# The first token tile scaled by ScalarE, two Sin calls moved into the layer, and the last tile routed ahead of its low part, in a two-layer hybrid transformer kernel on Trainium2

## What is computed

```python
for l in range(2):
    h = rms_norm(x, norm_mix_g[l])
    q, k_c, v_c, k_s, v_s, k_w, v_w, nsa_g, sgu_in, s5_in, branch_g = split(h @ w_in[l])
    y_a = nsa_attention(q, k_c, ..., positions, ...) @ w_attn_o[l]   # partial_rope: cos/sin of positions
    y_b = spatial_gating(sgu_in, ...) @ w_sgu_o[l]
    y_c = s5_layer(s5_in, ...) @ w_s5_o[l]
    g_a, g_b, g_c = split(sigmoid(branch_g))
    x = x + (g_a * y_a + g_b * y_b + g_c * y_c) @ w_mix_o[l]
    h = rms_norm(x, norm_ffn_g[l])
    # 4 groups x 8 experts, the best group, its best 2 experts per token, silu(h Wg) * (h Wu) @ Wd
    x = x + hierarchical_moe(h, ...)
return rms_norm(x, norm_final_g)
```

## Time and profile before

| | us |
|---|---|
| median of 3 runs | 1911.43 (1910.63 to 1912.46) |
| the profiled execution, its device time | 1910.96 |
| its span in the trace | 1909.2 |
| PE busy | 1848.6 (97%), 10376 records |
| DVE busy | 990.3 (52%) |
| ACT busy | 483.7 (25%) |
| POOL busy | 151.2 (8%) |
| mean granted TensorE clock | 0.99 of full |
| read from HBM | 476.59 MB |

### The profile page before, as it was taken

The page is one execution under the profiler, slowest core; times in us unless marked ns, Lnnn a source line. Parts: engine busy times, 40 slices in busy tenths (PEclk is TensorE's granted clock), DMA queues, the critical chain, the costliest instruction groups (busy, mean ns, idle before and its releaser), DMA issues. The chain is left out here.

```text
span 1909.2 us, 26714 instructions
## 1 busy us (share of the span) xinstructions
PE 1848.6 (97%) x10376; PEld 1156.9 (61%) x10377; DVE 990.3 (52%) x1929; ACT 483.7 (25%) x858; POOL 151.2 (8%) x241
## 2 busy tenths in 40 slices
PE   6999999999999999999889999999999999999996
PEld 3777777778545445454347877778775445455442
DVE  7755556667334343343478555567673344343344
ACT  4413444432111111111234234444321110111112
POOL 4600000050000000000054000000500000000000
PEclk9999999999999999999989999999999999999998
DMA  4222111344999999999722221114359999999994
GB/s 170 67 98 85 67 67 45 111 140 190 377 428 427 419 428 427 427 428 417 314 65 77 95 68 65 67 45 133 118 226 423 427 424 425 429 427 427 423 428 175
DMA packets 59952, 482.13 MB, mean 253 GB/s; under 512 B 9808, under 2 KB 22608, under 8 KB 30672
## 3 DMA queue, kind: packets, MB, share of 16 engines
q1 hardware_dynamic: 59856, 480.80, 62.1%
HBM read 476.59 MB, written 4.19 MB: 252 GB/s over the span
## 5 line engine op out<-in xcount | busy, mean ns | idle before, releaser
L1932 DVE TENSOR_TENSOR x_tokens<-x_tokens,ps 128x512 f32<-128x512 f32 x240 | 160.3, 686 | 216.5 <-PE ps L1084 215.5
L1109 PE MATMUL ps<-slabs,arena 128*64 128x512 f32 x512 | 228.4, 599 | 4.3 <-issue 4.3
L1110 PE MATMUL ps<-slabs,arena 128*64 128x512 f32 x512 | 228.4, 600 | 0.0
L1100 PE MATMUL ps<-arena,branch 128*64 128x512 f32 x512 | 227.0, 596 | 0.5 <-ACT branch L1403 0.5
L1100 PE MATMUL ps<-slabs,branch 128*64 128x512 f32 x512 | 227.0, 595 | 0.0
L1109 PE MATMUL ps<-arena 128*64 128x512 f32 x512 | 225.0, 592 | 0.9 <-DVE arena L1922 0.9
L1110 PE MATMUL ps<-arena 128*64 128x512 f32 x512 | 225.0, 592 | 0.0
L822 PE MATMUL ps<-h_hi,w_parts 128*128 128x512 f32 x768 | 210.8, 408 | 1.5 <-DVE w_parts L1545 1.5
L1109 PEld LDWEIGHTS ps<-slabs,arena 128*64 128x64 f32 x512 | 70.7, 138 | 151.9 <-issue 151.9
L822 PEld LDWEIGHTS ps<-h_hi,w_parts 128*128 128x128 f32 x768 | 135.1, 189 | 38.8 <-issue 9.2
L1109 PEld LDWEIGHTS ps<-arena 128*64 128x64 f32 x512 | 70.0, 137 | 145.8 <-issue 145.8
(11 more groups left out here) (361 smaller groups left out, 3094.0 us busy)
## 6 DMA issues: line engine op xcount, KB each, us to landing
arena<-in_expert_w_gate SPq DMA_DIRECT2D x32, 2048.0 KB, 12.1
slabs<-in_expert_w_gate SPq DMA_DIRECT2D x32, 2048.0 KB, 15.0
slabs<-in_expert_w_up SPq DMA_DIRECT2D x32, 2048.0 KB, 19.4
arena<-in_expert_w_up SPq DMA_DIRECT2D x32, 2048.0 KB, 16.5
arena<-in_expert_w_down SPq DMA_DIRECT2D x32, 2048.0 KB, 9.5
slabs<-in_expert_w_down SPq DMA_DIRECT2D x32, 2048.0 KB, 13.9
slabs<-in_gate_w SPq DMA_DIRECT2D x24, 1024.0 KB, 4.8
slabs<-in_dense SPq DMA_DIRECT2D x22, 1024.0 KB, 5.8
```

The costliest lines, as they stand in the source:

```text
L1100: done = nc.tensor.matmul(ps[64 * b:64 * b + 64, BANK_Y[half], :], hidT[:, k, CAP * b:CAP * (b + 1)], w_down[b][:, k, half * 512:(half + 1 ...
L1109: nc.tensor.matmul(ps[0:64, BANK_GU[b], :], xk, low[:, k, :], start=(k == 0), stop=(k == ND - 1), tile_position=(0, 0))
L1110: return nc.tensor.matmul(ps[64:P, BANK_GU[b], :], xk, high[:, k, :], start=(k == 0), stop=(k == ND - 1), tile_position=(0, 64))
L1932: v.tensor_tensor(xs, xs, ps[:, banks[n % len(banks)], :], ALU.add).then_inc(s["back_added"], 1)
```

## The change

In the order of the program:

- **First tile.** A new place `hT_first` (in memory that the layer uses only later) holds the transposed tile 0. ACT fills it by eight 128x128 copies from PSUM with gmix as the scale, one per channel block (`first_tile`): for layer 0 at the end of the prologue, for layer 1 at the end of layer 0's block (and, after an overflow, in the block that makes the turned tiles anew). PE's transposes of tile 0 tell ACT. DVE's loop at a layer's start has tiles 1 to 3 only, hT_ready counts them, and everything that reads tile 0 takes it from `tile_of(0)`.
- **Sins.** The two Sins over 128x512 angles leave the prologue and are made in layer 0 behind the layer's own two Sins; DVE's first use of them waits for both. The prologue has no load of that table.
- **PE's waits** on y_read are dropped in three places, where a wait on y_lo_ready stands beside each.
- **First experts' tokens.** Of each half (4 blocks) DVE moves two blocks in a 128x512 operation and ACT two blocks in two 128x256 copies with gffn as the scale; PE waits for ACT's count (xe_first) ahead of these blocks.
- **Routing.** `route(3)` stands ahead of `low_part(3, 0, 4)` on DVE.
- **Between the layers** the first of the two barriers around the clearing of the layer's semaphores is gone.

The SP queue's loads of weights are the same and in the same order.

```diff
+        hT_first = view(O_XS, ND, P)
+
+        def tile_of(t):
+            return hT_first if t == 0 else hT[:, :, t * P:(t + 1) * P]
...
-                nc.tensor.transpose(ps[:, BANK_X[t][d // 4], (d % 4) * P:(d % 4 + 1) * P], x_unit[:, t, d * P:(d + 1) * P], ident)
-
-        def turn_tokens(pe, g):
+                last = nc.tensor.transpose(ps[:, BANK_X[t][d // 4], (d % 4) * P:(d % 4 + 1) * P], x_unit[:, t, d * P:(d + 1) * P], ident)
+            return last
+
+        def first_tile(layer, told):
+
+            for d in range(ND):
+                nc.scalar.activation(hT_first[:, d, :], ps[:, BANK_X[0][d // 4], (d % 4) * P:(d % 4 + 1) * P], ACT.Identity,
+                                     scale=gmix[:, 8 * layer + d:8 * layer + d + 1]).then_inc(told, 1)
+
+        def turn_tokens(pe, g, told):
 
             for t in range(NT):
                 pe.wait_ge(g["xn"], t + 1)
-                turn_tile(t)
+                last = turn_tile(t)
+                if t == 0:
+                    last.then_inc(told, 1)
...
+        first_turned = so["ov_down"]
...
-                turn_tokens(pe, turn_g)
+                turn_tokens(pe, turn_g, first_turned)
...
                 square_tokens(act, turn_g, pro_x)
-                act.wait_ge(s["pro_dve"], N_REDUCE)
-                nc.scalar.activation(rope_sin, rr, ACT.Sin).then_inc(s["pro_act"], 1)
-                act.wait_ge(s["pro_dve"], 2 + N_REDUCE)
-                nc.scalar.activation(rope_cos, r2, ACT.Sin).then_inc(s["pro_act"], 1)
-                act.wait_ge(s["pro_act"], 2)
+                act.wait_ge(s["pro_gmix"], 16 * L)
+                act.wait_ge(first_turned, 1)
+                first_tile(0, first_turned)
...
+        shared = dict(xe_first="ov_hT_read", next_turned="ov_back", nsa_parted="ov_silu", outp_free="ov_weights", m_hi_ready="ov_sel", m_lo_ready="ov_gathered", br_hi_ready="ov_xe", br_lo_ready="ov_gu",
...
-                            last = nc.tensor.matmul(ps[r:r + 32, BANK_S[0], t * P:(t + 1) * P], wnsa[k], hT[:, k, t * P:(t + 1) * P],
+                            last = nc.tensor.matmul(ps[r:r + 32, BANK_S[0], t * P:(t + 1) * P], wnsa[k], tile_of(t)[:, k, :],
...
-                            last = nc.tensor.matmul(out[:, 0:hi - lo], hT[:, k, t * P:(t + 1) * P], w[:, k, lo:hi],
+                            last = nc.tensor.matmul(out[:, 0:hi - lo], tile_of(t)[:, k, :], w[:, k, lo:hi],
...
-                        pe.wait_ge(s["hT_ready"], t + 1)
+                        if t >= 1:
+                            pe.wait_ge(s["hT_ready"], t)
                         token_job(J_SGU + t, w_sgu, 0, S, t)
...
-                        pe.wait_ge(s["y_read"], 2 * i)
...
+                                if first and b == 0 and k % 4 >= 2:
+                                    pe.wait_ge(s["xe_first"], 2 * (k // 4) + k % 4 - 1)
...
-                            turn_tile(t)
+                            last = turn_tile(t)
+                            if t == 0:
+                                last.then_inc(s["next_turned"], 1)
...
+                    if layer == 0:
+                        nc.scalar.activation(rope_sin, rr, ACT.Sin).then_inc(s["pro_act"], 1)
+                        nc.scalar.activation(rope_cos, r2, ACT.Sin).then_inc(s["pro_act"], 1)
...
-                                act.wait_ge(s["hT_ready"], u + 1)
-                                nc.scalar.activation(h_hi[:, :, u * P:(u + 1) * P], hT[:, :, u * P:(u + 1) * P], ACT.Identity).then_inc(s["h_hi_ready"], 1)
+                                if u >= 1:
+                                    act.wait_ge(s["hT_ready"], u)
+                                nc.scalar.activation(h_hi[:, :, u * P:(u + 1) * P], tile_of(u), ACT.Identity).then_inc(s["h_hi_ready"], 1)
...
+                    for half in range(2):
+                        act.wait_ge(s["x_gathered"], half + 1)
+                        for k in (4 * half + 2, 4 * half + 3):
+                            nc.scalar.activation(xe[0][:, k, :], ps[:, BANK_GATHER0 + 2 * half + 1, (k % 2) * QUAD:(k % 2 + 1) * QUAD], ACT.Identity,
+                                                 scale=small["gffn"][:, k:k + 1]).then_inc(s["xe_first"], 1)
...
+                    if not last_layer:
+                        act.wait_ge(s["next_turned"], 1)
+                        first_tile(layer + 1, s["next_turned"])
...
-                    for t in range(NT):
+                    for t in range(1, NT):
...
-                        v.tensor_tensor(h_lo[:, :, cols], hT[:, :, cols], h_hi[:, :, cols], ALU.subtract).then_inc(s["h_lo_ready"], 1)
+                        v.tensor_tensor(h_lo[:, :, cols], tile_of(t), h_hi[:, :, cols], ALU.subtract).then_inc(s["h_lo_ready"], 1)
...
+                        if layer == 0 and i == 0:
+                            dve.wait_ge(s["pro_act"], 2)
...
                     inverse(3)
+                    route(3)
                     low_part(3, 0, 4)
-                    route(3)
                     placed(3)
...
-                        take(0, half, BANK_GATHER0 + 2 * half)
+                        v.tensor_tensor(xe[0][:, 4 * half:4 * half + 2, :], ps[:, BANK_GATHER0 + 2 * half, :].rearrange("p (b c) -> p b c", c=QUAD),
+                                        gf(4 * half, 2, QUAD), ALU.mult).then_inc(s["xe_ready"], 1)
...
-                clear(nc, layer_sems)
+                nc.sync.sem_clear(range(layer_sems[0].num, layer_sems[-1].num + 1))
+                nc.all_engine_barrier()
```

8 lines of the change are left out of this document (4 added, 4 removed).

## The result

The changed kernel takes 1895.49 us (median of 4, 1894.8 to 1897.16) against 1911.16 for the kernel before (median of 4). The ratio is 0.9919, with a 95% interval of 0.9905 to 0.9932: 15.7 us faster, where 6.0 were forecast and 1902.8 was the lower end of the range. The profiled execution took 1894.8 us, with a span of 1893.1.

What follows compares the result with a forecast made beforehand. PE, busy 1848.6 of 1909.2 us, was taken as the bound; 0.4 (prologue), 1.85 (routing), 1.9 (between layers) and 1.85 (second routing) sum to 6.0, giving 1905.4 us against the median, range 1902.8 to 1908.0.

Steps and rivals of the forecast that it cites:

- The prologue: Program start: ACT's eight copies replace both Sins and end at about 18.65 instead of 19.04, so layer 0 starts 0.4 us earlier.
- the upper bound given: Prologue: if the copies come faster than 0.28 us apart, PE's last transpose at 18.46 binds and 0.6 us is gained.
- Both routings: Routing of tile 3 in each layer: gather 1.37 us earlier plus 0.47 of the take's wait, 1.85 per layer.
- the idle stretch of the queue: Weight loads between 482 and 485: the queue moves nothing, so the stream can start earlier with PE and 1.85 us is kept.
- The low part of tile 3: Layer 0, sign of being right: PE still waits for this low part, at about 54.5.
- the waits on y_read cost 0: PE's dropped waits: y_lo_ready is awaited in the same places and comes after, so removal gives 0.
- The transition's 1.9: Between the layers: 0.5 us for the barrier and 1.44 for DVE's two operations, together 1.9 earlier.
- the room of 2.3 at the low part: Layer 1: low part of tile 3 ready at 1000.51, used at 1002.81; PE's lead takes 1.4 of 2.3, gain kept.
- The clock rival: Start of layer 1: shorter wait leaves PE's clock up, of 2.80 us only 0.9 could be kept, 1904.5 us; 12%.
- The load stream: Experts' stage, rival: last weights come when they came before, both routing gains of 1.85 are lost, 1909.1 us; 8%.
- The copies weren't long: Rival on ACT's copies from PSUM: slower than 0.28 us; at 1.0 each, 4.0 us slower, 1915.4; 3%.
- The first rival: Second layer's start limited by PE's weights or its way through the branch: only the barrier's 0.5 counts, 1906.8 us; 14%.

Runs made afterwards that it cites:

- b_noread: Kernel before with only PE's waits on y_read taken out in three places; 1901.33 us beside 1909.5, ratio 0.9961.
- a_reads: Changed kernel with PE's three waits on y_read put back; 1900.71 us beside 1909.5 for the kernel before, ratio 0.9959.
- a_again: Changed kernel once more, with nothing altered, for a second profile; 1893.87 us beside 1909.5 for the kernel before, ratio 0.9930.
- a_again2: Changed kernel once more, with nothing altered, on another chip; 1894.95 us beside 1908.9 for the kernel before, ratio 0.9927.
- a_nofirst: Changed kernel with tile 0 moved by DVE again, the Sins still moved; 1895.63 us beside 1908.66 for the kernel before, ratio 0.9936.
- a_noroute: Changed kernel with the half low part again ahead of route(3); 1899.29 us beside 1908.66 for the kernel before, ratio 0.9957.

## Why the prediction was wrong

**The direction and the terms that had a size hold.** The prologue: 0.4 forecast, 0.60 measured, because the copies came 0.25 apart and overlapped, and PE's last transpose bound it, the upper bound given. (The starts of layer 0 differ by more than that between profiles, 1.2 us among those of the changed kernel, so this agreement is worth little.) Both routings: 1.85 each against 1.99 and 1.97 from the logits to the gate product, and kept past the loads, as argued from the idle stretch of the queue. The queue's first load left at 480.26 instead of 484.80. The low part of tile 3 was what PE waited for in layer 0.

**The step that failed is that the waits on y_read cost 0.** As waits they do: PE has no other waits in the experts' stage with them than without. As instructions they don't. With them out, PE's branch past the overflow's code took 0.35 us instead of 3.68 and 3.45, worth 3.3 us between the layers and 2.6 at the end of the profile; alone they gave 7.4 us (b_noread), and put back they cost 5.8 to 6.8 (a_reads). That the branch's target then lay in what was already fetched is the reading that fits. The sum put a duration on every operation and none on the code itself.

**The step before it failed in the reading.** Between the layers PE stood for 7.26 us. I explained 1.44 of it by DVE and 0.5 by the barrier and took the other 5.3 as fixed, without asking what it was. The row of 3.6 for PE's queue at L2312 stands in the same view as the row of 0.5 that I used. Read, it would have been a rival: a branch that takes fifty times as long on PE as on the other engines (3.68 us against 0.05 to 0.07), and a change that shortens PE's program ahead of it.

**The transition's 1.9 came out near its size, by other ways.** Its two terms are there at the start of layer 1, 1.44 and 0.6. But the room of 2.3 at the low part was measured with PE's start at half clock for 16.77 us of two jobs and with in_bparam landing 2.9 after its issue. In the changed kernel's first profile PE's clock was back sooner (PE gained another 1.1 up to the low part) and the load landed 1.9 later; PE then waits 1.47, and 1.6 is lost again. In a_again and a_again2 the load landed 3.9 and 4.1 after its issue and PE waits 0.59 and 0.71. From the last transpose to the first product on h_lo, b_noread, which has the short branch and nothing else of the change, takes 40.31 us; the three profiles of the changed kernel take 39.17, 38.30 and 38.41, so 1.1 to 2.0 less, with some clock in it. That this lies around 1.9 is in part luck: a bonus of the clock and a later landing, neither in the sum, nearly cancel. The Trainium skill's page on the clock ("TensorE: Matmul & The Clock Gate"), as the prediction read it, has the slow stretch only move with PE. It didn't keep its length: PE worked 4.1 us at the low level at the start of layer 1 (956.72 to 960.85) where it had been 5.6 (966.06 to 971.70). The clock rival named both the bonus and this cap; the landing time it held constant.

**The clock at other places** was no term at all. The profile before has three stretches at half clock in busy work outside the transition (mix of layer 0, last expert of both layers), the changed kernel's has one. The three places before, and then now:

```profile
410.00:416.00 6.00, 3.57 (x11) 2.88 (x11) 1.22 (x1) 1.66 (x1) 6.00 (x5) 0.72 0.82 264
920.00:928.00 8.00, 6.03 (x21) 1.97 (x19) 0.69 (x1) 0.59 (x1) 0.00 (x0) 0.79 1.01 432
1866.00:1873.00 7.00, 4.70 (x16) 1.74 (x16) 0.69 (x1) 0.59 (x1) 0.00 (x0) 0.76 1.00 426
```

```profile
410.00:416.00 6.00, 4.81 (x21) 3.94 (x22) 2.33 (x2) 1.07 (x1) 5.94 (x5) 1.00 0.89 291
916.00:924.00 8.00, 5.53 (x19) 1.97 (x19) 0.69 (x1) 0.59 (x1) 0.00 (x0) 0.79 1.01 428
1854.00:1861.00 7.00, 5.87 (x28) 2.07 (x26) 0.69 (x1) 0.59 (x1) 0.00 (x0) 1.00 1.02 431
```

The one at 1866 cost the 1.70 of the table, the one at the mix 1.2 of its 1.87. They come and go between profiles: 4 of 18 have one at the mix of layer 0, after waits of 1.8 to 2.4 us, and others waited as long without one; a_nofirst alone has one at the mix of layer 1 (1348.57), after 1.88. This part of the profiled difference, about 3 us, is a draw and not the change's. What is the change's is the gather: 5 of 8 against 0 of 28.

**The rivals.** The load stream didn't take the gains. The copies weren't long. The first rival was right that PE's own way through the branch limits the second layer's start; but the change shortened that too, so the time went to the other side.

Put together, as an estimate for a typical execution of the changed kernel: 0.6 at the start, 3.9 in the routings, 5.9 of branches, 1.1 to 2.0 in the transition, and some 2 of clock at the gather (5 of 8 layers times two layers, 1.7 each) make 13.5 to 14.4, where the ratios of a_again and a_again2 stand for 13.4 and 13.9, and the first comparison for 15.5 (0.9919) with its interval from 13.0. Several of these terms scatter between profiles by 1 us, so the agreement shows no more than that nothing large is missing.

## What to carry to other kernels

Account for all of a gap that the change touches before costing a part of it, and read the waits of the queues (SPq, PEq) beside those of the engines: a meeting of all engines shows in one row who came last. A branch over code that isn't run can have a price that hangs on how long the program ahead of it is. Here a dozen instructions added or removed far ahead of it moved the time by some 3 us for each such branch, more than most of the edits were meant to give; so look at the long COMPARE_BRANCH rows after every edit. Where an engine's start is moved up, what it waits for next sets the gain: here eight copies and a new buffer were worth 0.2 to 0.8 us in the traces, and a swap of two lines 2.9 by itself (1.44 in each layer, a_noroute) and 5.8 with the clock in that profile.

## What the runs showed of the hardware that was not expected

- PE's taken branch over the overflow's code took 0.35 us with up to 10 instructions more ahead of it than in the changed kernel, and 3.4 to 3.7 with 13 or 14 more; with 9 or 10 more, PE stood for 2.5 and 2.7 us a few instructions behind the branch instead. The four other engines' branches at the same line took 0.05 to 0.07.
- A wait of PE of 1.7 us ahead of the last tile's rank was followed within a few us by a granted clock of 0.5 of full in 5 of 8 cases; without it, with 0.68 us at most, in none of 28. At the last expert PE waits 0.7 to 2.7 us: of the ten waits of 2.0 us or more five were followed by the low level, of the 26 shorter ones (up to 1.85) none. The trace doesn't say in advance which of the ten.
- The 256 KB load of in_bparam, issued at the layer's start, landed 2.8 to 3.2 us after its issue in layer 0 and 2.9 to 5.2 in layer 1, in profiles whose queue held the same loads.
